# Attention masks loaded one stage earlier, ScalarE's weight pieces served ahead of the exponentials, and GpSimd's whole-slab low parts in four instructions

## The reference

```
x = first_block(x, ...)                     # 2 layers: mixers, w_out, gated feed-forward
h = rms_norm(x) * (1 + scale) + shift
proj = h @ w_in                             # q, k, v of both attentions, gates, mixes
oa = nsa_attention(...)                     # 16 heads of 64, compressed + masked scores
ya = (oa * silu(za)) @ w_br_a
ob = dilated_mixture(...)                   # 8 heads of 128, masked scores
yb = (ob * silu(zb)) @ w_br_b
out = (sigmoid(ma) * ya + sigmoid(mb) * yb) @ w_out
```

## Time and profile before

| | |
|---|---|
| three runs | 3970.29, 3957.03, 3972.97 us; median 3970.29 |
| profiled execution | 3960.19 us, span 3958.4 us |
| mean granted TensorE clock | 0.965 of full speed |
| busy: PE, PEld | 3662.7 us (93%), 3249.1 us (82%) |
| busy: DVE, ACT, POOL | 2039.9 us (52%), 1771.8 us (45%), 1729.3 us (44%) |
| L193 on POOL | 20 instructions, 91.5 us |
| stage A, stage B | 3218 to 3446 us, 3490 to 3544 us |

### The profile page before, as it was taken

One profiled execution on the slowest core, in us unless ns is written; L12 is line 12 of the kernel. 1 busy time (PEld: TensorE's weight loads), 2 busy tenths in 40 slices (PEclk: granted clock), 3 DMA queues, 4 the chain that ended last, 5 costly groups with the idle time before them and its releaser, 6 DMA issues. The chain is left out here.

```text
span 3958.4 us, 60887 instructions
## 1 busy us (share of the span) xinstructions
PE 3662.7 (93%) x25724; PEld 3249.1 (82%) x25724; DVE 2039.9 (52%) x2013; ACT 1771.8 (45%) x1860; POOL 1729.3 (44%) x824
## 2 busy tenths in 40 slices
PE   8898899899999999898999899999998989889988
PEld 7788888788888887787888688888887788888877
DVE  4747533655555555647532655555555443344454
ACT  4415444544443444416444544443445345444434
POOL 0426565599991000425666499993000155530000
PEclk9999899999999999998999999999999999999999
DMA  5423345477775554423345477775554533335543
GB/s 190 138 66 123 117 144 187 160 239 240 240 239 176 185 186 130 146 67 110 122 128 181 157 244 245 238 238 179 183 190 165 167 121 118 111 128 179 170 152 125
DMA packets 378828, 655.47 MB, mean 166 GB/s; under 512 B 13713, under 2 KB 189921, under 8 KB 377745
## 3 DMA queue, kind: packets, MB, share of 16 engines
q1 hardware_dynamic: 363248, 596.98, 46.3%
q0 software_dynamic: 15392, 55.79, 4.2%
HBM read 645.37 MB, written 6.29 MB: 165 GB/s over the span
## 5 line engine op out<-in xcount | busy, mean ns | idle before, releaser
L214 PE MATMUL ps<-x_parts,w_hi 128*128 128x512 f32 x6160 | 2191.0, 400 | 89.8 <-DVE x_parts L1294 25.4
L215 PE MATMUL ps<-x_parts,w_lo 128*128 128x256 f32 x6160 | 1734.7, 282 | 0.0
L193 DVE TENSOR_TENSOR w_lo<-weight_ring,w_hi 128x2048 fp32r<-128x2048 f32 x392 | 950.1, 2424 | 1057.0 <-ACT w_hi L185 1056.8
L214 PEld LDWEIGHTS ps<-x_parts,w_hi 128*128 128x128 f32 x6160 | 1169.3, 190 | 382.3 <-issue 60.9
L185 ACT ACTIVATE w_hi<-weight_ring 128x2048 fp32r<-128x2048 f32 (+1 forms) x412 | 787.8, 1912 | 1168.3 <-PE ps L215 1108.4
L215 PEld LDWEIGHTS ps<-x_parts,w_lo 128*128 128x128 f32 x6160 | 1174.9, 191 | 0.0
L604 PE MATMUL ps<-x_parts,w_hi 128*128 128x256 f32 x2592 | 781.3, 301 | 68.3 <-ACT arena L622 34.2
L605 PE MATMUL ps<-x_parts,w_hi 128*128 128x256 f32 x2592 | 746.8, 288 | 0.0
L606 PE MATMUL ps<-x_parts,w_lo 128*128 128x256 f32 x2592 | 745.5, 288 | 0.0
L604 PEld LDWEIGHTS ps<-x_parts,w_hi 128*128 128x128 f32 x2592 | 510.7, 197 | 100.6 <-issue 57.6
L555 POOL TENSOR_TENSOR w_lo<-weight_ring,w_hi 128x1024 fp32r<-128x1024 f32 (+1 forms) x152 | 377.8, 2485 | 340.7 <-ACT w_hi L552 333.5
(11 more groups left out here) (403 smaller groups left out, 2840.7 us busy)
## 6 DMA issues: line engine op xcount, KB each, us to landing
weight_ring<-in_w_in SPq DMA_DIRECT2D x212, 1024.0 KB, 5.2
weight_ring<-in_w_ffn_gate SPq DMA_DIRECT2D x88, 1024.0 KB, 5.2
weight_ring<-in_w_ffn_up SPq DMA_DIRECT2D x88, 1024.0 KB, 5.2
weight_ring<-in_w_ffn_down SPq DMA_DIRECT2D x88, 1024.0 KB, 5.2
spare<-in_w_ada POOLq DMA_DIRECT2D x96, 512.0 KB, 4.4
weight_ring<-in_w_out SPq DMA_DIRECT2D x32, 768.0 KB, 4.6
weight_ring<-in_w_out SPq DMA_DIRECT2D x24, 1024.0 KB, 5.1
weight_ring<-in_w_br_a SPq DMA_DIRECT2D x8, 1024.0 KB, 5.1
```

The source lines that it names most:

```text
L193: (ops or core.nc.vector).tensor_tensor(core.w_lo[:, g % 2, at], core.ring[:, (self.start + g) % RING, at], core.w_hi[:, g % 2, at].bitcas ...
L214: mm(out, hi, core.x_parts[:, x, :, :].rearrange("p a t -> p (a t)"), start=first, stop=False)
L215: return mm(out[:, 0:T], lo, core.x_hi[:, x, :], start=False, stop=last)
```

## The change

Three things are changed. The masks' loads move from the attention stage to SP's queue at the head of the rotary stage before it; VectorE's wait for them stays where it was. The steps of an attention unit go from three to four: the pieces before the transposes are divided over two steps (3 becomes 2 + 1 in stage A, 2 becomes 1 + 1 in stage B), PE runs both at the same place as before, and ScalarE serves the first of the two ahead of the next unit's exponentials. And where GpSimd makes the low part of a whole slab, it does so in four instructions of a quarter each.

```diff
@@ Stream.low
-        at = slice(0, self.slot)
-        (ops or core.nc.vector).tensor_tensor(core.w_lo[:, g % 2, at], core.ring[:, (self.start + g) % RING, at],
-                                              core.w_hi[:, g % 2, at].bitcast(F32), ALU.subtract).then_inc(core.lo_ready, 1)
+        parts = 1 if ops is None else 4
+        for n in range(parts):
+            at = slice(n * self.slot // parts, (n + 1) * self.slot // parts)
+            last = (ops or core.nc.vector).tensor_tensor(core.w_lo[:, g % 2, at], core.ring[:, (self.start + g) % RING, at],
+                                                         core.w_hi[:, g % 2, at].bitcast(F32), ALU.subtract)
+        last.then_inc(core.lo_ready, 1)
@@ rope_stage, sync engine
+            for dst, src in loads:
+                tables.start(sp, dst, src)
             weave.sp(sp, len(jobs))
@@ attention_stage, sync engine
-            for dst, src in masks["loads"]:
-                load.start(sp, dst, src)
-            weave.sp(sp, 3 * len(units))
+            weave.sp(sp, 4 * len(units))
@@ attention_stage, tensor engine
                 if u + 1 < len(units):
                     score(u + 1)
-                weave.pe(pe, 3 * u)
+                weave.pe(pe, 4 * u)
+                weave.pe(pe, 4 * u + 1)
                 pe.wait_ge(*probs.at(u + 1))
...
-                weave.pe(pe, 3 * u + 1)
+                weave.pe(pe, 4 * u + 2)
...
-                weave.pe(pe, 3 * u + 2)
+                weave.pe(pe, 4 * u + 3)
@@ attention_stage, scalar engine
             def finish(u):
-                weave.act(act, 3 * u)
+                weave.act(act, 4 * u + 1)
...
                 s = shape(u % 2, L)
+                if u:
+                    weave.act(act, 4 * u - 4)
                 act.wait_ge(*tops.at(u + 1))
                 for x in range(N):
                     ins = nc.scalar.activation(s[:, x, :], s[:, x, :], ACT.Exp, bias=stats(u, x, 1), accum_out=stats(u, 8 + x, 1))
@@ attention_stage, vector engine
-            dve.wait_ge(*load.all())
+            dve.wait_ge(*landed.all())
@@
-ATTENTION_A_SHARES = ([8, 2, 1, 2], [0] * 4 + [1] * 12 + [2], [3, 2, 1] * 15 + [3, 2, 1, 128])
-ATTENTION_B_SHARES = ([0] * 4 + [1] * 12 + [2], [2, 2, 1] * 4 + [32])
+ATTENTION_A_SHARES = ([8, 2, 1, 2], [0] * 4 + [1] * 12 + [2], [2, 1, 2, 1] * 15 + [2, 1, 2, 1, 128])
+ATTENTION_B_SHARES = ([0] * 4 + [1] * 12 + [2], [1, 1, 2, 1] * 4 + [32])
```

More of the change, by code:

```diff
@@ L2851, in compress_stage, with rope_stage @@
     m.end()
-def rope_stage(m, tiles, rot, trig, turn, weave, keys=None, product=None):
+def rope_stage(m, tiles, rot, trig, turn, weave, keys=None, product=None, tables=None, loads=()):
     nc = m.nc
@@ L2927, in rope_stage, with attention_stage @@
     m.end()
-def attention_stage(m, units, masks, scale, s_at, pt_at, weave, cmp=None):
+def attention_stage(m, units, masks, scale, s_at, pt_at, weave, cmp=None, landed=None):
     nc = m.nc
@@ L2942, in attention_stage @@
         m.sig(n) for n in ("scores", "scores_read", "row_max", "exps", "weights", "v_turned", "v_ready", "o_done", "o_read"))
-    load = Load(m, "tables_landed")
     def shape(b, L):
@@ L2960, in _ @@
         def _(sp):
-            for dst, src in masks["loads"]:
-                load.start(sp, dst, src)
-            weave.sp(sp, 3 * len(units))
+            weave.sp(sp, 4 * len(units))
         @block.gpsimd
         def _(pool):
-            weave.pool(pool, 3 * len(units))
+            weave.pool(pool, 4 * len(units))
         @block.tensor
@@ L3019, in _ @@
                 mm.then_inc(*o_done.up())
-                weave.pe(pe, 3 * u + 2)
-            weave.pe(pe, 3 * len(units))
+                weave.pe(pe, 4 * u + 3)
+            weave.pe(pe, 4 * len(units))
         @block.scalar
@@ L3035, in finish @@
                 ins.then_inc(*stored.up())
-                weave.act(act, 3 * u + 1)
+                weave.act(act, 4 * u + 2)
             def put(u):
@@ L3042, in put @@
                 nc.scalar.activation(dst, m.ps[:, 4, 0:n * P].rearrange("p (a b) -> p a b", b=P), ACT.Copy).then_inc(*o_read.up())
-                weave.act(act, 3 * u + 2)
+                weave.act(act, 4 * u + 3)
             for u, (tt, items, _, _) in enumerate(units):
@@ L3059, in _ @@
             put(len(units) - 1)
-            weave.act(act, 3 * len(units))
+            weave.act(act, 4 * len(units))
         @block.vector
@@ L3178, in second_block @@
     vt = [m.flat(28 + 2 * b, 512).rearrange("p (a b) -> p a b", a=2) for b in range(2)]
+    masks = m.flat(32, 2 * T + 60)
+    cmask = [masks[:, 2 * T + 30 * tt:2 * T + 30 * tt + 30] for tt in range(2)]
+    add = [masks[:, tt * T:(tt + 1) * T] for tt in range(2)]
+    tables = Load(m, "tables_landed")
     beside_a.plan(ATTENTION_A_SHARES[1])
     rope_stage(m, tiles.each(0, 8), m.const("rot_a"), trig[:, 0, :, :], [(tiles.each(14, 2), vt[0]), (tiles.each(18, 2), vt[1])],
-               beside_a, keys)
+               beside_a, keys, tables=tables,
+               loads=[(x, m.const_dram(f"{n}{tt}")) for n, xs in (("causal", add), ("cmp", cmask)) for tt, x in enumerate(xs)])
     units = []
@@ L3192, in second_block @@
             units.append((tt, items, outs, m.arena[:, 52 + j:53 + j, tt * P:(tt + 1) * P]))
-    masks = m.flat(32, 2 * T + 60)
-    cmask = [masks[:, 2 * T + 30 * tt:2 * T + 30 * tt + 30] for tt in range(2)]
-    add = [masks[:, tt * T:(tt + 1) * T] for tt in range(2)]
     def cmp_scores(u, hh):
@@ L3201, in second_block @@
     beside_a.plan(ATTENTION_A_SHARES[2])
[L3202 to L3205, removed]
+    attention_stage(m, units, dict(add=add), HD ** -0.5, 36, 44, beside_a,
+                    dict(scores=cmp_scores, values=lambda u: vc[:, u // 4 * HD:(u // 4 + 1) * HD], mask=cmask, gates=gates), landed=tables)
     beside_a.end_weave()
@@ L3210, in second_block @@
     vtb = m.flat(8, 2048).rearrange("p (a b) -> p a b", a=2)
+    addb = [m.flat(32, T), m.flat(33, T)]
     beside_b.plan(ATTENTION_B_SHARES[0])
-    rope_stage(m, tiles_b[0:16], m.const("rot_b"), trig[:, 1, :, :], [(tuple(tiles_b[16:24]), vtb)], beside_b, product=(xa, oa, za))
-    addb = [m.flat(32, T), m.flat(33, T)]
+    rope_stage(m, tiles_b[0:16], m.const("rot_b"), trig[:, 1, :, :], [(tuple(tiles_b[16:24]), vtb)], beside_b, product=(xa, oa, za),
+               tables=tables, loads=[(addb[tt], m.const_dram(f"dilated{tt}")) for tt in range(2)])
     units = []
@@ L3221, in second_block @@
     beside_b.plan(ATTENTION_B_SHARES[1])
-    attention_stage(m, units, dict(add=addb, loads=[(addb[tt], m.const_dram(f"dilated{tt}")) for tt in range(2)]),
-                    P ** -0.5, 16, 24, beside_b)
+    attention_stage(m, units, dict(add=addb), P ** -0.5, 16, 24, beside_b, landed=tables)
     beside_b.end_weave()
```

## The result

| | before | after |
|---|---|---|
| median | 3970.39 us (3957.03 to 3980.02, 20 runs) | 3978.43 us (3971.57 to 3982.67, 20 runs) |
| profiled execution, span | 3960.19, 3958.4 | 3976.04, 3974.3 |
| stage A, 16 units | 233.69 | 242.55 |
| stage B, 4 units | 53.75 | 47.45 |

The ratio is 1.0021, 95% interval 1.0013 to 1.0029: 8 us slower, not 9 us faster. A stage is here the stretch from its first matmul to the first of the next stage, the same two matmuls in every kernel, so that its length can be compared wherever it lies.

What follows compares the result with a forecast made beforehand. PE was taken to bound the kernel, leaving only its idle and half-clock time to win. Stage A -5.8, stage B -5.5 and low parts +2.5 sum to -8.8: from 3970.29 to 3961 us, 8-in-10 range 3934 to 3984.

Steps and rivals of the forecast that it cites:

- The step that failed: Stage A, odd units: DVE's small and large weight products run through without GpSimd coming between; no loss, bounds 0 to 2.2 per unit.
- rival (2): Stage A: GpSimd also holds DVE's large product in odd units, +21.4 us, kernel 3983, slower than before; chance 0.17.
- Masks: Stage A's opening: with masks loaded early PE waits 0.95 us instead of 4.50 for the second scores, -3.6.
- Read waits: Stage A, four units: PE no longer waits for ScalarE's read of a finished woven pair, -15.4 us.
- Even units: Stage A, eight even units: GpSimd's earlier low part holds DVE's weight chain, PE waits 2.4 us each before the transposes.
- Odd units: Stage A, seven odd units: DVE is further along when GpSimd starts, so no loss was taken.
- Clock: Stage A, half-clock time: -2.4 behind the opening, -10.0 behind the read waits, +6.8 after new stalls.
- Stage B: Second attention stage: -3.4 opening wait, -2.8 clock, +0.7 for table loads around the exponentials; -5.5 us in all.
- Low parts: Whole-slab low parts in four: +3.0 at waits and stage ends, +2.0 at recurrent-input stages, gain in second rotary stage; +2.5.
- rival (3): Recurrent-input stages: GpSimd's quarter low parts starve behind an unbroken DVE series, twice, +11 us, kernel 3973; chance 0.10.
- the gain of 2.5 in the second rotary stage: Quartered low parts give DVE turns, so PE's 4.46 us wait becomes some 2.6 in three pieces: -1.9, clock -0.6.

Runs made afterwards that it cites:

- the swap: The whole change with DVE's last two normalising products of a unit swapped, large one ahead of the small: 3991.8 us, one run.
- the later start: The whole change, with GpSimd setting 32 spare columns and waiting for that before each attention-stage low part, so starting 0.18 us later: 3959.9 us, one run.
- odd units gated: The whole change, with GpSimd's low parts waiting for VectorE to finish the unit's weights in odd units alone: 3958.3 us, ratio 0.9968 to before.
- GpSimd 0.03 later: The whole change, with GpSimd setting one spare column before each attention-stage low part, moving its start 0.03 us: 3976.3 us, ratio 1.0034 to before.
- the gated kernel: The whole change, with GpSimd's low parts waiting in every unit until VectorE has made that unit's weights: 3939.0 us, ratio 0.9931 to before.

## Why the prediction was wrong

The prediction had 9 us faster by a stage A that is 5.8 us shorter; it is 8.9 longer, and the kernel 8 us slower.

**The step that failed** is the sentence "L3107 and L3109 are of the first kind, with no wait between: I take no loss here". The place and the price of the loss stood in rival (2), even the order of the starts (GpSimd 0.03 us after L3107; measured 0.03): I had two rows that disagreed and weighed the wrong one. The eight L1864 are a case in which DVE held through a series; they do not show that a series holds. The same trace of before had other plain pairs beside a low part, and in them GpSimd came in between:
```profile
348.71 0.28 DVE L1873 TENSOR_TENSOR arena<-arena 128x128 f32<-128x128 f32 x1
348.79 2.43 POOL L555 TENSOR_TENSOR w_lo<-weight_ring,w_hi 128x1024 fp32r<-128x1024 f32 x1 [7.81 <-ACT w_hi L552]
...
348.91 2.46 DVE L1874 TENSOR_TENSOR arena<-arena,h 128x128 f32<-128x128 f32 x1
...
372.43 0.28 DVE L1873 TENSOR_TENSOR arena<-arena 128x128 f32<-128x128 f32 x1
```
L1874, normally 0.28, took 2.46 when GpSimd started 0.08 us into the L1873 ahead of it. But GpSimd's start at 372.50 fell just so, 0.07 us into an L1873, and there the whole series ran first.
I had picked the row instead of listing all of its kind. Listed, the trace of before has ten starts of a low part during a plain two-tensor operation whose follower was then held, and eight after which DVE ran its series to the end. All eight are in the code of L1873, L1874 and L1864, four in each layer, and nine of the ten are there too.

The Trainium skill (SBUF — State Buffer, section "SBUF: two separate sides") says that the one that starts first gets the port pair "for the whole instruction", which I read as one instruction. The odd units agree, and so do the swap and, in the mirror, the later start, where the large product's 1.22 held GpSimd for 0.98. The eight series do not agree. Why they held is open, so that the runs show what happens at this seam and not what decides at every seam.

**By the terms of the sum, stage A** (idle and busy of PE in the table's profiles):
- Masks: predicted -3.6 of waiting; measured -3.3 (18.6 against 21.9), and the second scores wait 1.02 instead of the foretold 0.95. Right.
- Read waits: -15.4; all 15.7 are gone. Right.
- Even units: +18.8; measured 15.7, which is 1.97 each where 2.4 was forecast; the masks-only kernel has 0.7 of it too: +15.0. The hold had the size drawn (2.08), DVE's chain ended 0.17 sooner (6.54 after the scores' end, not 6.71), and PE came to the transposes 0.17 to 0.40 later (4.51 or 4.74, not 4.34).
- Odd units: 0; measured 7 x 1.84 = +12.9. Rival (2) had 15.4.
- Clock: -2.4 - 10.0 + 6.8 = -5.6. Measured by PE's busy time: -1.9 with the odd units gated, -0.5 in after. All the half clock of before cost 211.75 - 202.32 = 9.4 us, not the 12.4 that I gave back: that is some 19 us of busy PE at 1.2 GHz, and the rest of the 27 lay in PE's own waits, where it costs nothing. The new stalls' share, 209.84 - 202.32 = 7.5 for eight of them, fits the 6.8.

With odd units gated these add up to -5.4 against -5.8. The agreement is luck in part: the even units came 3.8 cheaper than forecast, and the clock gave back 3.7 less. The odd units then bring +14.3 (12.9 of waiting, 1.4 of clock), where rival (2) had +21.4: its clock was charged at 6 and came at 1.4.

**Stage B:** predicted -5.5, measured -6.3. The opening's second scores wait 0.92 (0.80), the clock is at 1.00 and brings 3.9 of PE's busy time (2.8 forecast), and there are two more table loads (eight in the stage, 1.28 each). PE's wait for the read behind the exponentials fell from 3.31 to 2.64, but the first transposes now wait 1.50 for L3114, where they had waited for nothing: +0.8 for the two, where +0.7 was forecast for the table loads alone.

**Low parts:** predicted +2.5; alone 0.9998 (0.9986 to 1.0010), that is -6 to +4 us. Their instruction cost is there, 103.5 us for 80 instead of 91.5 for 20, 0.6 us a slab. The waits that it was to lengthen did grow in the profile of after: the wait of 2.36 at 118 is 3.15 (+1.05 forecast), its twin in the second layer too, the one at 3167 is 1.45 instead of 1.02, all of PE's waits for L195 make 9.0 us instead of 5.7 for L193, and the four stage ends of L1342 14.5 instead of 13.6. The first slab's last part ended at 121.5 (121.8 forecast, 126 by rival (3), which is out). The kernel with the low parts alone has the same sums (8.9 and 14.5), and its interval does not exclude 4 us. What did not come is the gain of 2.5 in the second rotary stage. The wait of 4.46 in the second rotary stage was cut up, but into six, of which the two longest in a row are
```profile
3487.32 0.70 PE L2874 MATMUL ps<-h,small_consts 128*128 128x256 f32 x2 [0.86 <-DVE h L2931]
3490.62 0.70 PE L2874 MATMUL ps<-h,small_consts 128*128 128x256 f32 x2 [1.19 <-DVE h L2931]
```
and these six make 4.7, where three of 2.6 in all were forecast; the stretch stays at 38.7 us: cut, not shortened.

**Left open.** What the ratio gives beyond the two stages is +5 us for after (+8 in all, +2.6 in the stages), between -3 and +6 for the others, and +11 for the kernel with GpSimd 0.03 later. It follows no part of the change (masks only +4, order only -3, low parts only 0), and the intervals are 3 to 7 us to either side; its cause is open. The longer waits for the low parts are some 4 us of it in the profile of after, but the low parts alone have the same waits and a ratio of 0.9998.

## What to carry to other kernels

When a step is moved ahead, ask first whom it wakes. Here a split served early started GpSimd 2.8 instead of 6.3 us after the scores' end (unit 2), into DVE's tail, and 0.18 us of its start decided over some 15 us of stage A. Move only the operation that is waited for (the read) and leave what nobody needs yet, or make the second engine wait for the end of the first one's critical chain. And where one row says "held" and another "not held", list every pair of that kind before choosing.

## What the runs showed of the hardware

- A seam between two DVE instructions issued with no wait between them can let GpSimd in: in 7 of 7 odd units, after a product of 0.19 us and, swapped, after one of 1.22. It does not always: at eight places of before a series of DVE ran to its end first (GpSimd 5.77 instead of 2.39 at 372.50). Started 0.10 us after a DVE instruction, GpSimd waits for its end (3.36 for 2.38); started 0.07 us before, the DVE instruction waits for GpSimd's (3.42 for 1.22).
- The hold is about as long for a narrow operation as for a wide one: two columns took 2.09 instead of 0.17, 1024 columns 3.42 instead of 1.22.
- PE's stalls of 2 us in every unit of some 15 us left a granted clock of 0.96 in stage A, that is 0.04 x 2 x 242.6, some 19 us at 1.2 GHz; where its longest stall was 1.03 us (the gated kernel), the granted clock was 1.00 over all 206 us.
